# Two stacked transformer blocks on one core: layers written out, each layer's end preparing the next one's rows

## What is computed

```python
# block one, one layer (rms = RMS norm with a gain)
u = rms(h, g_mix_pre)
gq, gk, gv, gg, ra_f, ra_b, aq, ak, av, gate_a, gate_b = split(u @ w_in)
la_f, la_b = (log_sigmoid(ra @ w_alpha_up + b_alpha) / 16 for both directions)
branch_a = (rms(gla(gq, gk, gv, la_f) + gla_reversed(..., la_b), g_gla_out) * silu(gg)) @ w_o_gla
branch_b = attention(rope(rms(aq)), rope(rms(ak)), av) @ w_o_attn
mixed = sigmoid(gate_a) * branch_a + sigmoid(gate_b) * branch_b
h = h + rms(mixed @ w_out, g_mix_post)
gate, up = split(rms(h, g_ffn_pre) @ w_ffn_in)
h = h + rms((silu(gate) * up) @ w_ffn_out, g_ffn_post)
h = h + rms(sigmoid(h @ w_ple_gate) * (p_i @ w_ple_proj), g_ple_post)

# block two, one layer
x = x + 0.5 * swiglu(rms(x, ffn1_norm), ffn1_w_in, ffn1_w_out)
rx, rgate, q, k, v, f, ga, gb = split(rms(x, mix_norm) @ w_in)
x = x + (sigmoid(ga) * rglru_branch(rx, rgate) + sigmoid(gb) * forgetting_attention(q, k, v, f)) @ w_o
x = x + 0.5 * swiglu(rms(x, ffn2_norm), ffn2_w_in, ffn2_w_out)
x = x + sigmoid(rms(x, ple_norm) @ ple_w_gate + ple_b_gate) * (p_i @ ple_w_proj)
# and a last rms(x, final_norm) after both layers
```

## Time and profile before

| | us |
|---|---|
| median of 3 runs (2432.20 to 2435.16) | 2433.78 |
| the profiled execution | 2436.17 |
| its span, first to last instruction | 2434.5 |
| TensorE busy in it | 2330.2 |

### The profile page before, as it was taken

One profiled execution on the slowest core, in us unless ns is written; L12 is line 12 of the kernel. 1 busy time (PEld: TensorE's weight loads), 2 busy tenths in 40 slices (PEclk: granted clock), 3 DMA queues, 4 the chain that ended last, 5 costly groups with the idle time before them and its releaser, 6 DMA issues.

```text
span 2434.5 us, 39760 instructions
## 1 busy us (share of the span) xinstructions
PE 2330.2 (96%) x15696; PEld 2143.5 (88%) x15696; DVE 1453.6 (60%) x1609; ACT 1228.1 (50%) x1633; POOL 35.8 (1%) x60
## 2 busy tenths in 40 slices
PE   7999999979999999989999899999899999999997
PEld 6879899868889899789898799998799897899986
DVE  4865654466755654555566766555555568656555
ACT  4764544465654544554447745444544448544444
POOL 1000000000000000010000000000100000000000
PEclk9999999999999999989999999999999999999999
DMA  6525465545335555555564355554465554355553
GB/s 221 175 67 181 163 202 181 184 154 173 122 118 177 189 183 182 173 170 191 174 198 130 114 191 183 190 190 173 158 197 189 192 163 156 122 182 183 184 174 128
DMA packets 322723, 412.46 MB, mean 169 GB/s; under 512 B 9264, under 2 KB 244784, under 8 KB 322528
## 3 DMA queue, kind: packets, MB, share of 16 engines
q1 hardware_dynamic: 318048, 395.40, 48.6%
q0 software_dynamic: 4336, 13.67, 1.8%
q10 hardware_dynamic: 144, 0.73, 0.1%
HBM read 408.72 MB, written 1.05 MB: 168 GB/s over the span
## 4 chain that ended last, share of the span: by engine, by line
PE 75%; DVE 8%; ACT 7%; issue 6%; DMA 4%; ACTq 0%; SPq 0%; DVEq 0%
PE bank L530 16%; PE bank L532 16%; PE bank L531 16%; PE bank L582 7%; PE bank L583 7%; PE bank L584 7%; DMA raw<-in_w_in 3%; DVE lo L1547 3%; ACT hi L1032 3%; ACT prob L1217 1%; DVE y L2018 1%; ACT hjunk L1244 1%; PE bank L628 0%; DMA raw<-in_w_ffn_in 0%; DMA raw<-in_ple_w_gate 0%
## 5 line engine op out<-in xcount | busy, mean ns | idle before, releaser
L1547 DVE TENSOR_TENSOR lo<-raw,hi 128x2048 fp32r<-128x2048 f32 (+1 forms) x384 | 861.6, 2247 | 702.2 <-ACT hi L1032 701.0
L1032 ACT ACTIVATE hi<-raw 128x2048 fp32r<-128x2048 f32 (+1 forms) x384 | 719.0, 1873 | 362.5 <-DMA raw<-in_w_in 124.5
L530 PE MATMUL bank<-x_in,hi 128*128 128x256 f32 x3072 | 874.0, 285 | 6.1 <-DVE lo L1547 6.0
L532 PE MATMUL bank<-x_in,lo 128*128 128x256 f32 x3072 | 871.5, 284 | 0.0
L531 PE MATMUL bank<-x_in,hi 128*128 128x256 f32 x3072 | 871.4, 284 | 0.0
L530 PEld LDWEIGHTS bank<-x_in,hi 128*128 128x128 f32 x3072 | 591.2, 192 | 8.5 <-DVE lo L1547 5.1
L531 PEld LDWEIGHTS bank<-x_in,hi 128*128 128x128 f32 x3072 | 591.3, 192 | 0.1
L532 PEld LDWEIGHTS bank<-x_in,lo 128*128 128x128 f32 x3072 | 591.1, 192 | 0.0
L582 PE MATMUL bank<-hi,x_hid 128*128 128x512 f32 x528 | 206.1, 390 | 0.0
L584 PE MATMUL bank<-hi,x_hid 128*128 128x512 f32 x528 | 205.8, 390 | 0.0
L583 PE MATMUL bank<-lo,x_hid 128*128 128x512 f32 x528 | 205.7, 390 | 0.0
(11 more groups left out here) (310 smaller groups left out, 2736.2 us busy)
## 6 DMA issues: line engine op xcount, KB each, us to landing
raw<-in_w_in SPq DMA_DIRECT2D x106, 1024.0 KB, 5.1
raw<-in_ffn_w_in SPq DMA_DIRECT2D x88, 1024.0 KB, 5.0
raw<-in_w_ffn_in SPq DMA_DIRECT2D x44, 1024.0 KB, 5.1
raw<-in_ffn_w_out SPq DMA_DIRECT2D x40, 1024.0 KB, 5.0
raw<-in_w_ffn_out SPq DMA_DIRECT2D x20, 1024.0 KB, 5.0
raw<-in_w_o_gla SPq DMA_DIRECT2D x8, 1024.0 KB, 4.8
raw<-in_w_o_attn SPq DMA_DIRECT2D x8, 1024.0 KB, 4.8
raw<-in_w_out SPq DMA_DIRECT2D x8, 1024.0 KB, 4.9
```

The lines of the kernel that those rows point to most:

```text
L530: pe.matmul(to, wh[:, k, cut], x[:, k, 0, :], start=(k == 0), stop=False)
L532: mm = pe.matmul(to, wl[:, k, cut], x[:, k, 0, :], start=False, stop=(k == tile.kc - 1))
L1032: act_fn(high, of, ACT.Copy).then_inc(hi_done.up(), 1)
L1547: tt(rest, of, parts(tile, hi)[0].bitcast(F32), ALU.subtract).then_inc(lo_done.up(), 1)
```

## The change

- The loops are gone: the four layers are straight code on every engine. `line_of` appends the first two tiles of the next layer to a layer's list, and each layer's end makes them and multiplies them (`rows_in_turn`, `by_halves`); the next layer starts at its third tile.
- Block one's norms leave the root to the results: rows are only multiplied with the gain (`with_gain`) and turned, and `heads_in`, `times_root`, `gates_in` and `values_out` multiply the products with the root, as block two did before.
- Block one's jobs start with half of gv (`gva`, form A), then ra, gq, gk, the rest of gv.
- The product `e` moves from behind ffn1_out to behind wo, where its two halves stand between the turns; its result `et` has a place of its own. At ffn1_out's end the rows of `h` are turned token half by token half, between the products of pg.
- In block two, pg's last tile is done for t = 0, then two of the next layer's turns, then t = 1; after it `by_halves` multiplies the first half of the features of two tiles while the second half is still made.
- Cosines and sines aren't kept in `cst`: in every layer of block one GpSimd loads them into `rope_c` and `rope_s` (four more transfers, `par_in` 10 instead of 6), where VectorE multiplies them in place.

```diff
+            row(0, dram["g_mix_pre"][0], 0)
+            for layer in range(DEPTH):
                 enter("pool", 1, layer)
-                row(0, dram["g_mix_pre"], layer, -4)
-                pool.wait_ge(*row_in[0].at(1))
-                row(2, dram["g_ffn_pre"], layer, -2)
...
+                for a in range(2):
+                    for to, c in ((rope_c, C_COS), (rope_s, C_SIN)):
+                        pool.dma_start(to[:, a, :, :].rearrange("p t d -> p (t d)"),
+                                       dram["consts"][:, c:c + T * HD]).then_inc(par_in.up(), 16)
```

```diff
+            def by_halves(tiles, x, b, start, half, turns):
+                parts_of = []
+                for i, tile in enumerate(tiles):
+                    pe.wait_ge(*lo_done.at(tile.index + 1))
+                    take(b + i)
...
+                    if i == 0:
+                        pe.wait_ge(*turn_hi.at(start + half))
+                    for f in range(2):
...
+                        if i == 0 and f == 0:
+                            pe.wait_ge(*turned.at(start + half))
...
+                        for u in turns.get((i, f), ()):
+                            turn_one(*u)
+                pe.wait_ge(*turn_hi.at(start + 4))
...
+            def rows_in_turn(tiles, x, banks, start, first_turns, third, fourth):
+                for u in first_turns:
+                    turn_one(*u)
+                take(*banks)
+                for t in range(T):
+                    for i, tile in enumerate(tiles):
+                        if t == 0:
+                            pe.wait_ge(*lo_done.at(tile.index + 1))
+                        else:
+                            turn_one(*(third, fourth)[i])
+                        pe.wait_ge(*turn_hi.at(start + 2 * t + i + 1))
+                        mm = rows_a(tile, x, bank[banks[t]][:], t, i == 0, i == 1, [turned.at(start + 2 * t + i + 1)])
```

TensorE, between wo and ffn1 of block one, and at the ends of the layers:

```diff
-                ffn(BY1, "ffn1", 0, turn(xn, next_xn))
-                ple(BY1, lambda: turn(h, lambda u: h_ready.at(4 + u + 1)))
+                turn_one(0, 0, 0)
+                turn_one(0, 1, 1)
+                ple_rows(e, 0, (4, 5))
+                turn_one(1, 0, 2)
+                ple_rows(e, 1, (6, 7))
+                turn_one(1, 1, 3)
+                pe.wait_ge(*turn_hi.at(3))
+                form_b(BY1["ffn1_in"][0], x_in, 0, (turn_hi.at(4), turned.at(4)))
...
+                rows_in_turn(pg[0:2], x_a, (0, 1), 4, [(0, 1, 5, h_ready.at(6), h)], (1, 0, 6, h_ready.at(7), h),
+                             (1, 1, 7, h_ready.at(8), h))
+                last_two(pg[2:4], x_a, (2, 3), True)
+                if layer + 1 < DEPTH:
+                    rows_in_turn(ahead, x_in, (0, 1), 8, high_turns[:2], *high_turns[2:])
+                else:
+                    for u in high_turns[:3]:
+                        turn_one(*u)
+                    by_halves(ahead, x_in, 0, 8, 3, {(0, 0): high_turns[3:]})
...
+                rows_a(pg[3], x_a, bank[2][:], 0, False, True).then_inc(first_rows.up(), 1)
+                if layer + 1 < DEPTH:
+                    for u in by_features[:2]:
+                        turn_one(*u)
+                rows_a(pg[3], x_a, bank[3][:], 1, False, True).then_inc(tile_used.up(), 1)
+                if layer + 1 < DEPTH:
+                    by_halves(ahead, x_in, 0, 12, 2, {(0, 1): by_features[2:3], (1, 0): by_features[3:]})
```

The start of a layer of block one, on ScalarE and VectorE:

```diff
+                pump(ra[0].index)
+                act.wait_ge(*tile_used.at(gva[1].index + 1))
+                root_row_out(4)
+                act.wait_ge(*root_ready.at(0))
+                values_out(v1, 0, (0, 1))
+                pump(gq[1].index)
...
+                pump(ra[0].index)
+                dve.wait_ge(*par_in.at(10))
                 dve.wait_ge(const_in.sem, const_in.unit)
```

More of the change, by code:

```diff
@@ L424, in _ @@
                     load(tile, dram[w1[tile.job]], layer)
-            with sync.Fori(0, DEPTH) as layer:
+            for layer in range(DEPTH):
                 enter("sp", 2, layer)
@@ L644, in roots_to_row, with ffn @@
                 freed[b] = root_out.next()
-            def ffn_raw(by, tag, use, turn, turn_banks, first_bank, between):
+            def ffn(by, tag, use, first_bank, done, roots, later=(), between=()):
                 tiles = by[f"{tag}_in"]
@@ L720, in ple @@
-                mm.then_inc(tile_used.up(), 1)
-                for b in banks:
-                    freed[b] = et_ready.next()
-                late = turned_in()
-                ready = None
-                if where.part == 2:
-                    pe.wait_ge(*turned.at(14))
-                    def ready(tile):
-                        if tile.k0:
-                            pe.wait_ge(*turned.at(16))
-                job_a(by["pg"], x_in, [(0, 1), (2, 3)], ready, late)
-            def mix_out(by, part, after_ga, after_gb=None, between=None):
+                cut = slice(n * 512, (n + 1) * 512)
@@ new lines, in ple_rows @@
+                for t in range(T):
+                    take(banks[t])
+                    to = bank[banks[t]][:]
+                    for k in range(2):
+                        xh, xl = x_ple[:, k, 0, t * P:(t + 1) * P], x_ple[:, k, 1, t * P:(t + 1) * P]
+                        pe.matmul(to, xh, wh[:, k, cut], start=(k == 0), stop=False)
+                        pe.matmul(to, xh, wl[:, k, cut], start=False, stop=False)
+                        mm = pe.matmul(to, xl, wh[:, k, cut], start=False, stop=(k == 1))
+                    freed[banks[t]] = et_ready.next()
@@ new lines, in _ @@
+                take(2, 3)
+                last_two(pg[2:4], x_a, (2, 3), True)
[3 more added lines that the diff above has]
+                    for u in high_turns[:3]:
+                        turn_one(*u)
+                    by_halves(ahead, x_in, 0, 8, 3, {(0, 0): high_turns[3:]})
+            by_features = [(0, 0, 4), (1, 0, 5), (0, 1, 6), (1, 1, 7)]
+            for layer in range(DEPTH):
+                enter("pe", 2, layer)
+                ahead = line_of(2, layer)[-AHEAD:]
+                ffn(BY2, "ffn1", 0, 0, 2, (4, root_ready.at(0)), by_features[:2])
+                turn_one(0, 1, 6)
@@ new lines, in _ @@
+                for t in range(T):
+                    square(bank[2 + t][:], psum[:, t, 0:1], squared)
+                act.wait_ge(*act_step.now())
+                for t in range(T):
+                    act_fn(pbias[:, t:t + 1], psum[:, t, 0:1], ACT.Identity, scale=1.0 / D,
+                           bias=head_eps[:, t:t + 1]).then_inc(act_step.up(), 1)
+                last_rows(ffn_out, 0)
+                square(bank[0][:], psum[:, 0, 1:2], squared)
+                root(0, psum, pbias)
@@ L1383, in _ @@
+                turned_high(x_a, 0, 0, 4)
+                last_rows(ffn_out, 1)
+                square(bank[1][:], psum[:, 1, 1:2], squared)
+                root(1, psum, pbias)
+                h_ready.next(4)
+                turned_high(x_a, 0, 1, 5)
+                turned_high(x_a, 1, 0, 6)
+                turned_high(x_a, 1, 1, 7)
                 warm(ACT.Sigmoid)
```

975 lines of the change are left out of this document (484 added, 491 removed).

## The result

| | before | after |
|---|---|---|
| median of 10 runs each, us | 2434.77 (2432.20 to 2436.17) | 2443.02 (2439.11 to 2444.66) |
| the profiled execution | 2436.17 | 2440.72 |
| its span | 2434.5 | 2438.7 |

The change makes the kernel slower: ratio 1.0033, 95% interval 1.0023 to 1.0042. I had forecast 2419, and the result lies above my range.

The account below looks back on a forecast made before the run. With TensorE busy 96% of the span and its products unchanged, only its stops and slower clock could move the time. Terms summed to -14.5: 2421.7 from the profiled 2436.17, 2419 us as median; range 2400 to 2433.

Parts of the forecast that it names:

- wo to ffn1: Block one, twice: rows turned with only the gain, covered by e; stop of 8 us becomes 1.3, -6.7 each, -13.4.
- ffn1_out to pg: Block one, twice: pg's own halves cover the turns of h; as much idle as before, 0, bounds -2 and +3 each.
- VectorE in block one: Some 28 more operations a layer make tiles late between decays and rope: +1.2 each, +2.4, bounds 0 and +11.
- (b): Start of block one's second layer: VectorE waits for par_in before the fourth tile's lo; +13.5.
- the slow rival: Start of block one's second layer: five transfers each wait for room in GpSimd's queue, up to +27, 2446; chance 0.07.
- My upper bound of +35: Bound on the second layer's start, if each of five larger transfers first waited as the 5.4 us of L482.
- The estimate of 2.6: Landing time in us of pt's 256 KB by the skill's formula; the forecast used the profile row's 3.3 us instead.
- (a): Start of block one's layers: the fourth tile's hi stands behind root row and values; +2.8 in the first layer.
- Ends of layers: Smaller stops at block one's first layer end (-9), block two's first to second layer (-9), block one to two (-2.5).
- the chain that I had called bare: Block one to two: form B tiles need both token halves, so nothing covers t = 1; first product at E+9.4, -2.5.
- my sign for this term (under 5): Telltale for block two's layer end: a window over it should lose under 5 us, from 12.4.
- The launch: Kernel start: tile one 2 us later behind 1.5 MB more of rows, tile two 2 earlier; +3, bounds -2 and +6.

Follow-up runs that it names:

- e6: The change with ScalarE's hi and VectorE's lo of pg's third tile, and VectorE's lo of its second, made earlier; ratio to before 0.9999.
- e4: The change with the second half of aq on banks (0, 3) in place of (3, 0); ratio to before 1.0004.
- e3: The change with cosines and sines loaded once in place of twice, two transfers of 128 KB fewer; ratio to before 1.0026.
- e1: The change with VectorE's wait for par_in and the rope tables moved behind the first product of gq; ratio to before 0.9983.
- e2: The change with block one's second-layer parameters loaded during ffn1_out (layer_done given earlier) and GpSimd's three rows behind them; ratio to before 0.9980.
- e5: The change with ScalarE's hi of the fourth tile (gq's first) ahead of the root row and the values; ratio to before 1.0033.
- e9: e5 plus VectorE scaling rat right behind ra's product, ahead of the lo of gq's second tile; ratio to before 1.0023.
- e7: The change with GpSimd's gain rows 2, 3 and 1 at the launch held back until row 0 has landed; ratio to before 1.0017.

## Why the prediction was wrong

For the profiled executions I had forecast -14.5, and the traces show +4.3: a miss of 18.8 us. By the prediction's own steps:

- **wo to ffn1: right.** -13.4 predicted, -12.9 measured, the window has a clock of 1.00 where it had 0.72, and the idle behind `xn` that was 4.8 us is 0.9.
- **"ffn1_out to pg ... 0, bounds -2 and +3 each": the step that failed most.** +4.2 and +5.8, more than half of the miss and outside its bounds. I counted the waits for pg's second tile and one copy and left out its third tile. In the order of ScalarE its `hi` stood behind three turned copies and a table load; I followed only what stood behind the gain of t = 1. e6 moved the two tiles and took the cost away: 0.5 each, and 8 us less in the time.
- **"VectorE in block one ... +1.2 each": wrong in kind.** 5.1 and 2.8. Predicted was +2.4, measured 7.9. I priced more work on VectorE, spread out. e4 shows that most of it (3.9 and 4.0) was one wait for a bank: rope was as late as ever, and the change had gg's first bank freed second. No count of VectorE's work could have shown that; the pairs of banks in the code do.
- **Start of the second layer, (b) +13.5: right mechanism, too small.** +16.4, and 1.1 in gv. The wait, its releaser and its place were as predicted; `layer_done` came 3 us later and the queue took 2.6 more. I had a pause of that kind as the slow rival, five times over; it came once, 4.0 us, until the transfers ahead had landed (e3). (My upper bound of +35 doesn't hold its own terms either: 13.5 and five times 5.4 make 40.5.) e1 and e2 confirm the term from two sides. On `pt` alone, 3.4 us passed from issue to landing, as the earlier trace rows had it. The estimate of 2.6 from the Trainium skill, DMA: Bandwidth & Descriptors (Anatomy of one DMA), is below that.
- **(a) +2.8: right, and not worth what it seemed.** The stop was 2.95 us. e5 removed nearly all of it and gained nothing, since the next wait stood 8 us behind; with e9 it was 2 us by the medians.
- **Ends of layers: right in sign, too large.** -6.5 for -9, -5.5 for -9 and -1.5 for -2.5. At the end of block one's first layer five waits of 0.5 to 1.5 us remain, for single normed rows and turned copies; from block one to two one of 6.3 us for `xn`, the chain that I had called bare, and two of under 0.8; from layer to layer of block two three of 0.5 to 2.3. In block two I had 12.4 lost and 3.4 of it left, and 6.9 are left, so my sign for this term (under 5) was missed. No run separates what the straight code gave here from what the new order gave.
- **The launch, +3 with bounds -2 and +6: right in kind.** The profiled execution shows +3.2 to the end of gv, with the 2.8 of (a) in it, and other executions +6.7 to +7.8. e7 shows that the rows were the cause of the late start.
- **A reading that changed nothing.** 46 matmuls in 10 us are one in 0.217 us, not 0.227, and 85 are one in 0.118. The paces that I used, 0.227 and 0.120, are nevertheless those of whole tiles: at equal work a tile takes 5.45 and 5.8 us.
- **Not foreseen: -8.9 and +3.2 in block two.** Before, TensorE waited 2.2 us in the gate products for ScalarE, which had a tile's `hi` and a table load in front of it:

```profile
1306.42 5.38 PE L970 MATMUL bank<-y,bd 128*128 128x256 f32 x16 [2.17 <-ACT ii L1449]
```

After, the tile is made earlier, the wait is gone, and the clock stays up. Some 4 of the 6.1 us in the first of block two's layers fall there. The +3.2 of the last layer's heads goes with a wait for `qkt` of 2.8 us where there was one of 1.9, and a clock of 0.89 behind it. All this seems a by-product of the moment at which tiles arrive; no edit touched it, so the cause isn't shown, and I can't say that another change would keep it.

**Median against profile.** The medians are 8.3 us apart and the profiled executions 4.6. The profile of before was its slowest run, that of the changed kernel one of its quicker, and the launch shows the second of these. Here are the changed kernel and e4, whose code is the same there, in windows over the stop before gq and over the decay product:

```profile
36.00:50.00 14.00, 11.05 (x77) 10.01 (x75) 7.49 (x5) 7.20 (x5) 0.00 (x0) 1.00 0.69 224
50.00:60.00 10.00, 10.00 (x84) 9.95 (x84) 9.97 (x14) 4.70 (x3) 0.00 (x0) 1.00 0.62 208
```

```profile
36.00:50.00 14.00, 11.05 (x66) 10.65 (x65) 7.33 (x5) 7.39 (x5) 0.00 (x0) 0.76 0.71 229
50.00:60.00 10.00, 10.00 (x60) 9.30 (x59) 9.53 (x12) 1.91 (x1) 0.00 (x0) 0.83 0.59 195
```

The same stop of 2.95 us at the same place, and one execution keeps the higher level while the other falls to the lower one twice, 11 and 24 instructions fewer in the same time. To the end of gv that is +3.2 against +7.5; e1, e2 and e6 have +7.3, +6.7 and +7.8. So the typical launch probably costs some 4 us more than the profile shows, and with it my terms for it (5.8) were too small too. There is one trace of before, so how much its own launch varies isn't known. Of the start of a kernel the Trainium skill says, in TensorE: Matmul & The Clock Gate (Part 1: The HAM clock gate), that the number of slow matmuls varies between runs of one kernel; these windows show such a difference behind a stop.

## What to carry to other kernels

Where a change moves the making of tiles, walk every tile near a seam through all its makers, not the first one that is late: TensorE stands for the last, and here it was the third tile. Read which bank the next product takes and which half frees it. A wait put ahead of supply work costs all that stands behind it (12 to 13 us here, by e1 and e2), and the same wait behind three tiles' `lo` found its transfers landed (e1), so place waits late before making transfers fewer. A stop that is removed alone may give nothing (e5): follow the chain to the next wait for the same supply before pricing it.

## What was unexpected of the hardware

- With a stop of 2.95 us in it, the launch kept the higher clock level in one execution (1.00 and 1.00 in the two windows) and had 0.76 and 0.83 in another, worth about 4 us. Short stops have no fixed price.
- GpSimd paused 4.0, 4.7 and 6.7 us (the change, e3, e2) in the middle of a row of small transfers, 7 or 8 transfers after the memset, with no releaser in the profile. In each case it went on 0.40 to 0.43 us after the last transfer issued ahead of the pause had landed. Before, with six, the longest pause at this place was 0.22.
